# High and low parts side by side in the moving operand of a recurrence's outputs and state updates

## The reference, cut to what matters

```
S_t = diag(f_t) S_{t-1} + k_t v_t^T        # state, 128 x 128 for each head
o_t = S_t^T q_t                            # output
o   = rms_norm(o) * silu(z)                # per head, over 128 channels
```

## Time and profile before

| | us |
|---|---|
| median of 3 runs (1290.31 to 1291.3) | 1290.8 |
| the profiled execution | 1290.74 |
| its span, first to last instruction | 1288.9 |
| TensorE busy | 1279.2 |
| VectorE busy | 726.0 |
| ScalarE busy | 689.4 |
| GpSimd busy | 498.9 |

### The profile page before, as it was taken

One profiled execution on the slowest core, in us unless ns is written; L12 is line 12 of the kernel. 1 busy time (PEld: TensorE's weight loads), 2 busy tenths in 40 slices (PEclk: granted clock), 3 DMA queues, 4 the chain that ended last, 5 costly groups with the idle time before them and its releaser, 6 DMA issues.

```text
span 1288.9 us, 16219 instructions
## 1 busy us (share of the span) xinstructions
PE 1279.2 (99%) x6297; PEld 1073.6 (83%) x6297; DVE 726.0 (56%) x1321; ACT 689.4 (53%) x1031; POOL 498.9 (39%) x207
## 2 busy tenths in 40 slices
PE   9999999999999999999999999999999999999998
PEld 7888888888887888888888888888878888888886
DVE  6656556552138456565768377777656556642442
ACT  5535544543235657666447577777655545462422
POOL 4553433434444332322335534434333333334530
PEclk9999999999999999999999999999999999999999
DMA  5732332324332232332243322222223222225411
GB/s 176 274 119 95 91 98 86 103 87 164 98 101 95 86 105 69 98 97 65 66 160 99 115 82 66 82 82 66 82 82 101 72 88 74 91 99 204 163 57 66
DMA packets 42589, 132.32 MB, mean 103 GB/s; under 512 B 6992, under 2 KB 9744, under 8 KB 42000
## 3 DMA queue, kind: packets, MB, share of 16 engines
q1 hardware_dynamic: 36416, 115.36, 28.0%
q10 hardware_dynamic: 6096, 15.92, 3.5%
HBM read 124.97 MB, written 10.49 MB: 105 GB/s over the span
## 4 chain that ended last, share of the span: by engine, by line
PE 93%; DVE 4%; ACT 1%; DMA 1%; issue 1%; POOL 0%; SPq 0%; DVEq 0%; ACTq 0%
PE banks L509 28%; PE banks L511 28%; PE banks L510 28%; PE banks L716 2%; PE banks L708 1%; PE banks L697 1%; DVE ylo L1748 1%; DMA raw<-w 1%; PE banks L623 1%; PE banks L936 1%; DVE nfull L1744 1%; ACT whi L1097 0%; PE banks L968 0%; PE banks L967 0%; DVE acc L1612 0%
## 5 line engine op out<-in xcount | busy, mean ns | idle before, releaser
L499 POOL TENSOR_TENSOR wlo<-raw,whi 128x1024 fp32r<-128x1024 f32 (+2 forms) x198 | 487.9, 2466 | 718.2 <-ACT whi L1097 717.8
L509 PE MATMUL banks<-hhi,whi 128*128 128x512 f32 x736 | 292.9, 398 | 0.2 <-DVE hlo L1795 0.2
L511 PE MATMUL banks<-hlo,whi 128*128 128x512 f32 x736 | 287.2, 390 | 0.0
L510 PE MATMUL banks<-hhi,wlo 128*128 128x512 f32 x736 | 287.1, 390 | 0.0
L1097 ACT ACTIVATE whi<-raw 128x1024 fp32r<-128x1024 f32 (+2 forms) x198 | 205.3, 1038 | 148.8 <-PE banks L511 86.7
L509 PE MATMUL banks<-yhi,whi 128*128 128x512 f32 x464 | 182.8, 394 | 0.7 <-ACT mcg L1471 0.5
L511 PE MATMUL banks<-ylo,whi 128*128 128x512 f32 x464 | 180.9, 390 | 0.0
L510 PE MATMUL banks<-yhi,wlo 128*128 128x512 f32 x464 | 180.7, 389 | 0.0
L511 PEld LDWEIGHTS banks<-hlo,whi 128*128 128x128 f32 x736 | 138.2, 188 | 29.3
L509 PEld LDWEIGHTS banks<-hhi,whi 128*128 128x128 f32 x736 | 138.5, 188 | 25.4 <-DVE hlo L1795 1.0
L510 PEld LDWEIGHTS banks<-hhi,wlo 128*128 128x128 f32 x736 | 138.6, 188 | 24.5
(11 more groups left out here) (389 smaller groups left out, 2177.4 us busy)
## 6 DMA issues: line engine op xcount, KB each, us to landing
raw<-w SPq DMA_DIRECT2D x193, 512.0 KB, 3.5
rel_tab<-relx ACTq DMA_DIRECT2D x1, 4096.0 KB, 19.5
tab<-rel_tab SPq DMA_DIRECT2D x16, 224.0 KB, 3.5
x<-xt ACTq DMA_DIRECT2D x1, 2048.0 KB, 8.7
x_kept<-x ACTq DMA_DIRECT2D x1, 2048.0 KB, 7.4
parts_kept<-mcg SPq DMA_DIRECT2D x8, 256.0 KB, 4.3
mgt<-parts_kept SPq DMA_DIRECT2D x8, 256.0 KB, 3.7
x<-x_kept ACTq DMA_DIRECT2D x1, 2048.0 KB, 8.3
```

Of the source, the lines that this page charges most:

```text
L499: nc.gpsimd.tensor_tensor(lo[:, begin:width], raw[:, n % 2, begin:width], f32(hi[:, begin:width]), ALU.subtract).then_inc(lo_done, 1)
L509: nc.tensor.matmul(dst, a[0], b[0], start=first, stop=False)
L510: nc.tensor.matmul(dst, a[1], b[0], start=False, stop=False)
L511: return nc.tensor.matmul(dst, a[0], b[1], start=False, stop=last)
```

## The change

The high and the low part of a moving operand are put next to each other in one tensor, so that high·high and high·low are one matmul of 256 columns with one stationary operand; low·high stays a matmul of 128 columns. A triple of 128 columns becomes a pair (256, 128). The result has twice the columns: the low product lies beside the high one and has to be added by another engine. This is done to the states of the outputs (`hss`), to the queries (`hqbs`) and to the values in the updates (`hv`, whose heads are interleaved by parts). The outputs of a head now fill banks 3 and 5.

What goes with it: ScalarE copies the low halves of the outputs out of PSUM (`hg_low`, two copies of 256 columns, into `hb`), VectorE adds the high halves (`hg_sum`, two additions of 256 columns, behind `qlo` and ahead of `qblo`), and squares and norm read `hb`. ScalarE's first cut of a head stands between `hg_low` and `hg_square`. Each of three state steps has an addition more. The score blocks run in the order 1, a part of 3, 0, the rest of 3 and 2, and block 0 waits for `hg_sum` of the head before, since it writes bank 5. Behind the last head the banks of `dn` 3 to 5 change, the squares and the sums are made earlier (the sums between the steps of `dn` 5), ScalarE's last `ml_silu_z` goes ahead of its last `hg_square`, and VectorE makes `mean` and `inv` before `turn`, and `diag` between the second and third crossing.

```diff
-DN_BANK = (1, 0, 2, 5, 4)
+DN_BANK = (1, 0, 2, 4, 6)
...
-            hqbs = [sb(n, [P, 2, TT - 1, P], F32R, scope) for n in ("hqbhi", "hqblo")]
+            hqbs = sb("hqbs", [P, 2, TT - 1, 2, P], F32R, scope)
...
-            hss = [sb(n, [P, S], F32R, scope) for n in ("hshi", "hslo")]
+            hss = sb("hss", [P, TT, 2, P], F32R, scope)
...
-        hv = [u[:, 0:KT, :].rearrange("p h (t v) -> p h t v", v=P) for u in (yhi, ylo)]
+        hv = [u[:, 0:KT, :].rearrange("p (h j) n -> p h (j n)", j=2).rearrange("p h (t c v) -> p h t c v", c=2, v=P)
+              for u in (yhi, ylo)]
+        head_out = [[(yhi, ylo)[u // TT][:, 2 * (u % TT) + c, :] for u in range(HH)] for c in range(2)]
...
+        out_pairs = [bank[3 if t < 2 else 5][:, (t % 2) * 2 * P:(t % 2 + 1) * 2 * P] for t in range(TT)]
+        update_pairs = [bank[4][:, 0:2 * P], bank[4][:, 2 * P:S], bank[3][:, 0:2 * P]]
+        out_split = [bank[b].rearrange("p (t c v) -> p t c v", c=2, v=P) for b in (3, 5)]
+        hb_parts = [hb[:, i * 2 * P:(i + 1) * 2 * P].rearrange("p (t v) -> p t v", v=P) for i in range(2)]
...
+                if k == 4:
+                    pe.wait_ge(hpV.sem, hpV.at("qlo", s))
+                    if s >= 1:
+                        pe.wait_ge(htV.sem, htV.at("far1", s - 1))
+                    hg_block(s, 1)
+                if k == 5:
+                    hg_block(s, 3, slice(CROSS, CROSS + P))
+                if k == 6:
+                    if s >= 1:
+                        pe.wait_ge(hoV.sem, hoV.at("sum", s - 1))
+                    hg_block(s, 0)
+                if k == 7:
+                    hg_block(s, 3, slice(0, CROSS))
+                    if s >= 1:
+                        pe.wait_ge(mzA.sem, mzA.at("z", s - 1))
+                    hg_block(s, 2).then_inc(htP.did("scores"), 1)
...
-                last = mm3(bank[4][:, t * P:(t + 1) * P], [u[:, t, :] for u in hkts], [u[:, s, t, :] for u in hv], True,
-                           True)
+                values = hv[s // TT][:, s % TT, t, :, :]
+                nc.tensor.matmul(update_pairs[t], hkts[0][:, t, :], values, start=True, stop=False)
+                last = nc.tensor.matmul(update_pairs[t][:, 0:P], hkts[1][:, t, :], values[:, 0, :], start=False, stop=True)
...
-                t = k // 2
-                cols = slice(t * P, (t + 1) * P)
+                t, to = k // 2, out_pairs[k // 2]
                 if t == 0:
                     pe.wait_ge(htV.sem, htV.at("slo", s))
+                    pe.wait_ge(htV.sem, htV.at("st3", s))
                     if s >= 1:
-                        pe.wait_ge(hoV.sem, hoV.at("norm", s - 1))
-                last = mm3(bank[3][:, cols], [u[:, s, t, :] for u in hv], [u[:, cols] for u in hss], True, t == 0)
+                        pe.wait_ge(hoV.sem, hoV.at("sum", s - 1))
+                values = hv[s // TT][:, s % TT, t, :, :]
+                nc.tensor.matmul(to, values[:, 0, :], hss[:, t, :, :], start=True, stop=False)
+                last = nc.tensor.matmul(to[:, 0:P], values[:, 1, :], hss[:, t, 0, :], start=False, stop=t == 0)
                 if t >= 1:
                     if t == 1:
                         pe.wait_ge(htV.sem, htV.at("stlo", s))
                         pe.wait_ge(hpV.sem, hpV.at("qblo", s))
-                    last = mm3(bank[3][:, cols], [u[:, t - 1, :] for u in hsts], [u[:, s % 2, t - 1, :] for u in hqbs],
-                               False, True)
+                    nc.tensor.matmul(to, hsts[0][:, t - 1, :], hqbs[:, s % 2, t - 1, :, :], start=False, stop=False)
+                    last = nc.tensor.matmul(to[:, 0:P], hsts[1][:, t - 1, :], hqbs[:, s % 2, t - 1, 0, :], start=False,
+                                            stop=True)
...
-            slab("dn", 3, bank[5], h)
+            slab("dn", 3, bank[4], h)
             hg_square(s)
-            slab("dn", 4, bank[4], h)
-            pe.wait_ge(hoV.sem, hoV.at("norm", s))
-            slab("dn", 5, bank[3], h)
+            slab("dn", 4, bank[6], h)
+
+            def down_sums(k):
+                if k not in (2, 3, 6, 7):
+                    return
+                g, first = k // 4, 2 * (k % 2)
+                if k == 2:
+                    pe.wait_ge(hoA.sem, hoA.at("ln", s))
+                    pe.wait_ge(dnV.sem, dnV.at("q2"))
+                if k == 6:
+                    pe.wait_ge(dnV.sem, dnV.at("k1"))
+                for b in (first, first + 1):
+                    tok = nc.tensor.matmul(bank[3][:, g * TT + b:g * TT + b + 1], dsq[:, (0, QL)[g], b * P:(b + 1) * P],
+                                           ones[:, 0:1], start=True, stop=True)
+                if k == 7:
+                    tok.then_inc(dnP.did("tok"), 1)
+
+            slab("dn", 5, bank[5], h, between=down_sums)
...
-            pe.wait_ge(hoA.sem, hoA.at("ln", s))
             pe.wait_ge(mzA.sem, mzA.all())
-            slab("g0", 0, bank[7], h, between=down_sums)
+            slab("g0", 0, bank[7], h)
             pe.wait_ge(dnV.sem, dnV.at("diag"))
-            for g, b in enumerate((6, 3)):
-                wide = nc.tensor.matmul(bank[b], ones, ddiag[:, g, :], start=True, stop=True)
-            wide.then_inc(dnP.did("wide"), 1)
+            nc.tensor.matmul(bank[3], ones, ddiag[:, 0, :], start=True, stop=True)
+            pe.wait_ge(dnV.sem, dnV.at("sum"))
+            nc.tensor.matmul(bank[5], ones, ddiag[:, 1, :], start=True, stop=True).then_inc(dnP.did("wide"), 1)
             pe.wait_ge(mcA.sem, mcA.at("gate", 0))
             pe.wait_ge(hoV.sem, hoV.all())
-            slab("pa", 0, bank[7], y_lower)
+            slab("pa", 0, bank[7], head_out)
...
+            def hg_low(u):
+                act.wait_ge(htP.sem, htP.at("o", u))
+                act.wait_ge(hpV.sem, hpV.at("four", min(u + 1, HH - 1)))
+                if u >= 1:
+                    act.wait_ge(hoV.sem, hoV.at("norm", u - 1))
+                for got, to in zip(out_split, hb_parts):
+                    low = nc.scalar.activation(to, got[:, :, 1, :], ACT.Copy)
+                low.then_inc(hoA.did("low"), 1)
+
             def hg_square(u):
                 if u >= 1:
                     act.wait_ge(hoV.sem, hoV.at("ylo", u - 1))
-                act.wait_ge(htP.sem, htP.at("o", u))
-                nc.scalar.activation(ho[:, 0, :], bank[3], ACT.Square).then_inc(hoA.did("sq"), 1)
+                act.wait_ge(hoV.sem, hoV.at("sum", u))
+                nc.scalar.activation(ho[:, 0, :], hb[:, :], ACT.Square).then_inc(hoA.did("sq"), 1)
                 act.wait_ge(hoA.sem, hoA.at("sq", u))
...
+                    hg_low(u)
+                cut()
+                if u >= 0:
                     hg_square(u)
-                cut()
                 if s >= 0:
...
+            def down_square(t):
+                used("dn", t)
+                nc.scalar.activation(dsq[:, t, :], bank[DN_BANK[t]][:, :], ACT.Square).then_inc(dnA.did(f"sq{t}"), 1)
+
+            hg_low(HH - 1)
+            ml_silu_z(HH - 1)
             hg_square(HH - 1)
+            for t in range(QL):
+                down_square(t)
...
             hg_root(HH - 1)
-            ml_silu_z(HH - 1)
             cut()
+            for t in range(QL, QL + KL):
+                down_square(t)
...
+            def hg_sum(u):
+                dve.wait_ge(hoA.sem, hoA.at("low", u))
+                for got, to in zip(out_split, hb_parts):
+                    last = V.tensor_tensor(to, got[:, :, 0, :], to, ALU.add)
+                last.then_inc(hoV.did("sum"), 1)
+
             def hg_norm(u):
                 dve.wait_ge(hoA.sem, hoA.at("root", u))
-                V.scalar_tensor_tensor(ho[:, 0, :], bank[3], cols("hg_g", 1)[0], ho[:, 1, :], ALU.mult,
+                V.scalar_tensor_tensor(ho[:, 0, :], hb[:, :], cols("hg_g", 1)[0], ho[:, 1, :], ALU.mult,
...
-                V.tensor_copy(hst[:, 0, :], bank[4][:, 0:P]).then_inc(htV.did("st1"), 1)
-                for n in (1, 2):
-                    dve.wait_ge(htV.sem, htV.at(f"st{n}", s))
-                    V.scalar_tensor_tensor(hst[:, n, :], hst[:, n - 1, :], hfac[:, n, 7:8], bank[4][:, n * P:(n + 1) * P],
-                                           ALU.mult, ALU.add).then_inc(htV.did(f"st{n + 1}"), 1)
+                for n, got in enumerate(update_pairs):
+                    if n == 0:
+                        V.tensor_copy(hst[:, 0, :], got[:, 0:P]).then_inc(htV.did("half1"), 1)
+                    else:
+                        dve.wait_ge(htV.sem, htV.at(f"st{n}", s))
+                        V.scalar_tensor_tensor(hst[:, n, :], hst[:, n - 1, :], hfac[:, n, 7:8], got[:, 0:P], ALU.mult,
+                                               ALU.add).then_inc(htV.did(f"half{n + 1}"), 1)
+                    dve.wait_ge(htV.sem, htV.at(f"half{n + 1}", s))
+                    V.tensor_tensor(hst[:, n, :], got[:, P:2 * P], hst[:, n, :], ALU.add).then_inc(htV.did(f"st{n + 1}"), 1)
...
+                    hg_sum(r - 1)
```

(31 more changed lines are left out.)

68 lines of the change are left out of this document (19 added, 49 removed).

## The result

| | before | after |
|---|---|---|
| median of 8 runs each | 1290.85 (1290.26 to 1291.48) | 1294.72 (1293.67 to 1295.62) |
| profiled execution | 1290.74 | 1295.62 |
| its span | 1288.9 | 1293.8 |

All times are us. The changed kernel takes 1.003 of the time before [1.0021, 1.004], 3.9 us more. The forecast was 1293.7.

The account below looks back on a forecast made before the run. TensorE looked like the bound, but a ring of waits through VectorE and ScalarE, 0.2 us behind, would bind: +1.7 to the down projections and +1.2 behind the last head, +2.9 on 1290.74, gives 1293.7 us; range 1284.5 to 1299.

Parts of the forecast that it names:

- The ring: Waits from `qlo` through scores, VectorE and ScalarE to the next `qlo`: 0.55 us more a head, 28.67, six heads, +3.3.
- Behind the last head's `qlo`: After the last wait TensorE is the bound again and saves one head's work: -1.1 us, leaving +1.7 to the down projections.
- TensorE's saving: Pairs for triples in outputs and updates: 0.11 us each, 1.1 a head, 8.9 in all if TensorE stays the bound.
- TensorE's busy time: Sign that the forecast is right: TensorE's busy time over the kernel down by about 9 us.
- Where TensorE stands: TensorE waits 1.5 to 1.7 us at the first score block, released by `qlo`, in each of six heads.
- GpSimd: Its subtraction beside `hg_sum` costs zero, at the other end 2.1 us; `qblo` would be held where nobody waits.
- The tail: From the end of `dn` 5 to `pa` 0, 11.4 us with lengthened `dn` 5 against 10.26: +1.2; bounds -1.5 to +2.
- The clock: Idle TensorE might have its clock lowered, shown as 1.2 GHz granted; judged unlikely, nothing in the sum.
- rival C: `hg_sum` caught by GpSimd, up to 2 us on six heads, 1300 to 1306, or TensorE's clock lowered; chance 0.10.
- A: Rival: TensorE stays the bound throughout and the whole 8.9 us show, 1283 us; chance 0.18.
- B: Rival: the ring binds but hardly grows, 27.9 to 28.3 us a head, 1288 to 1291.5; chance 0.17.

Follow-up runs that it names:

- e5: Changed kernel plus two more additions of 256 columns on VectorE between `qlo` and `hg_sum` of every head but the last: 1299.76 us, ratio 1.0068.
- e6: Changed kernel plus one addition of 512 columns on VectorE behind `qblo`, outside the ring: 1294.73 us, ratio 1.0032.
- e10: e7 plus the two additions of e5 between `qlo` and `hg_sum`: 1283.19 us, ratio 0.9943 to the kernel before.
- e1: Changed kernel with the square and its rounding behind `kthi` on ScalarE, its low part behind `ktlo` on VectorE: 1289.51 us, ratio 0.9989.
- e3: Kernel before the change with ScalarE's fourth cut of a head moved behind `hg_decays`: 1290.97 us, ratio 0.9999.
- e8: Changed kernel with the edits of e1, e2 and e7 together (square late, fourth cut late, gate early): 1282.2 us, ratio 0.9936.
- e7: Changed kernel with the fourth cut behind `hg_decays` and the gate of `g0` 0 ahead of `kp`: 1282.51 us, ratio 0.9939.
- e2: Changed kernel with ScalarE's fourth cut of a head moved behind `hg_decays`: 1284.87 us, ratio 0.9949 to the kernel before.
- e9: Changed kernel with only GpSimd's subtraction for `mz` of heads 1 to 7 held until `qlo` of the same head: 1284.95 us, ratio 0.9958.

## Why the prediction was right, and where it was off

The mechanism and the size of a head were right, and the time came out 1.0 us above the forecast. That it came so near is in part luck: outside the six heads two terms were wrong by 0.9 and 0.55 us in opposite directions, and a clock term was missing.

- **The ring.** Forecast 28.67 a head, measured 28.68. Its working holds term by term: `hg_sum` in its plain 0.75, the square at its end, `ktlo` and the copies without idle. From head 1's `qlo` (745.72 before, 745.42 after) to the last (914.44 and 917.49) the shift between the kernels goes from -0.30 to +3.05 us. That is a growth of 3.35, forecast 3.3, from a start forecast at -0.5. e5, e6 and e10 show the ring by doses, e1 by taking the square out.
- **Behind the last head's `qlo`.** The forecast took 1.1 us back here, since TensorE would be the bound again. From +3.05 the shift falls only to +2.62 (the last head's sum of squares, 945.64 before and 948.26 after), that is by 0.43. The pairs of that head save their 0.9 to 1.0, but the wait for `mz`'s gate comes a seventh time, at 922.95, and there no ring hides it (0.58). So the recurrence ends 2.62 later, forecast +1.7.
- **TensorE's saving.** This term was slightly too large. I took 0.11 us a pair, 1.1 a head; e3 and e8 give 28.12 - 27.14 = 0.98 a head, 0.10 a pair. It was hidden by the ring, as the prediction said, so it did no harm. The 27.0 of TensorE's work should have been 27.1 to 27.2, and its standing 1.5 us a head. TensorE's busy time fell by 3.0, and not by about 9 as the prediction had among its signs, because matmuls run on into the waits and TensorE ran at half the clock for 3 us; in e7, without these waits, it is 1270.5, 8.7 less than before.
- **Where TensorE stands.** The prediction named one wait of 1.5 to 1.7 us at the first score block. There are two of about half that, for `qlo` and for `mz`'s gate at the last block. That second wait was not in the text: the gate stands between the table load and `kthi` on ScalarE, so it slipped with them. Inside the ring it costs nothing of its own, because the scores, released by it, end together with `ktlo`; e1 took it away with the square. In the last head it costs what it lasts.
- **GpSimd.** `hg_sum` was not held and `qblo` was, at no cost. But the prediction looked only at the operations that the change adds, and took the ring's other lengths as given. `hd` at 2.70 was in all eight heads of the kernel before too, 2.0 us of it not work, and it decides what the change is worth: with it 3.9 us slower, without it (e2) 6.1 us faster.
- **The tail.** This term was mis-sized by a misread row. The prediction put the end of `dn` 5 at 957.67, but the sums that start there stand behind the first step of `g0` 0, as `between` is called behind a step. `dn` 5 ends one step of 0.68 earlier, at 956.99, and from there to `pa` 0 are 10.94 us and not 10.26. The same stretch of the changed kernel was forecast at 11.4 and takes 11.6 (from 959.61, which is eight plain steps behind the start of `dn` 5 at 954.17, to 971.20). So the tail grew by 0.65 (the shift goes from 2.62 to 971.20 - 967.93 = 3.27), and with the right row the prediction's own sum would have said +0.5 where it says +1.2. Its working behind the row held: the wait at `pa` 0 is 2.4, forecast 2.5.
- **The clock.** Not in the sum: 1.6 us in half of the executions behind the wait of 2.36. The prediction had it as part of rival C and judged it unlikely. It accounts for most of the 1.0 us that the median lies above the forecast: the four executions without it have a median of 1293.9. For the profiled execution the sum closes: 2.62 + 0.65 + 1.6 = 4.9, and 1295.62 - 1290.74 is 4.9.
- **The rivals.** A (TensorE stays the bound, 1283) was refuted by the two waits in each head, but its price was that of the kernel without the ring: e7 has 1282.5, with the gate early as well. B did not come, since the 0.57 a head was no artefact of gaps. C's catch of `hg_sum` did not come.

One thing isn't settled: which other condition decides whether the clock drops behind the wait at `pa` 0. That the wait is needed is shown (none of the 26 executions without it has a mean clock under 0.999, 20 of the 40 with it have), but the same wait shows the drop in some executions and not in others, and no kernel was made to find out why.

## What to carry to other kernels

Before a change that takes work off the busiest engine, find the second bound: follow the waits once around a period and add up the ring's length, here 0.2 us below TensorE's. Then look for operations in that ring that last longer than their size asks for; one of them, held by another engine, was worth more than the whole change. Check against the kernel's text which instruction a row belongs to before a sum starts from it: one step of 0.68 us taken for the wrong slab mis-sized the tail here. A dose of known length put inside and outside the supposed ring settles in two runs which of them binds.

## What was not expected of the hardware

- GpSimd's subtraction of 128 x 1024 and VectorE's operations with two SBUF inputs exclude each other in both directions. Where VectorE runs such operations back to back, the subtraction waits: in e7 it is issued at 822.67 and VectorE's rows run at their plain durations until 826.85, where `qblo` is caught. When it gets in it adds 1.5 to 2.2 us to an operation of VectorE (`qblo` 2.09 for 0.55, the square's low part 2.88 for 0.68), so only the place can be chosen. In e7 the catch lengthens the way from `qlo` to the copies to 6.82 us (825.32 to 832.14), where the changed kernel has 6.29 (860.11 to 866.40). From the copies to the next `qlo` are 20.36, which is the changed kernel's 22.39 less the 2.03 of `hd`: the ring has no idle time left to give. VectorE and GpSimd in that kernel:

```profile
825.32 0.95 DVE L2056 TENSOR_TENSOR hqxlo<-hqx,hqxhi 128x768 fp32r<-128x768 f32 x1
...
826.85 2.09 DVE L2061 TENSOR_TENSOR hqbs<-hqb,hqbs 128x384 fp32r<-128x384 f32 x1
828.87 2.88 DVE L1946 TENSOR_TENSOR hsqlo<-ho,hsqhi 128x512 fp32r<-128x512 f32 x1
...
832.14 1.96 DVE L1984 COPY_PREDICATED hs<-hm,banks 128x384 f32<-128x384 uint32 x8
...
852.50 0.95 DVE L2056 TENSOR_TENSOR hqxlo<-hqx,hqxhi 128x768 fp32r<-128x768 f32 x1
...
822.67 8.53 POOL L506 TENSOR_TENSOR wlo<-raw,whi 128x1024 fp32r<-128x1024 f32 x2 [6.88 <-ACT whi L1114]
```

- One wait of 2.36 us of a TensorE that was busy before it was followed by matmuls at 1.2 GHz for 3.2 us or more (971.20 to past 974.35) in some executions, and in others not at all. In e9 the first matmuls behind the same wait (from 962.89 to 964.19) still started 0.22 to 0.34 us apart, and the spacing of 0.43 came only behind them. The wait of 1.00 in the kernel before was not followed by one.
